# A hybrid decoder trunk on one Trainium2 core: rotary halves exchanged by GpSimd's DMAs, the decay from an exponential, the head norm from columns

## What is computed

```python
proj = rmsnorm(x, g) @ w_in       # rnn_gate, rnn_in, q, k, v, g_a, g_b: 7 x 1024 columns
u = causal_depthwise_conv(rnn_in)
r, i_gate = sigmoid(u @ w_a + b_a), sigmoid(u @ w_x + b_x)
a = exp(-8 * r * softplus(-lam))
h = scan(a, sqrt(1 - a * a) * i_gate * u)
y_a = h * gelu(rnn_gate)
# per head, q and k: t * cos + concat(-t[32:], t[:32]) * sin
w = softmax(q1 k1) - lam * softmax(q2 k2)      # 8 heads
y_b = rmsnorm(w @ v, g_sub) * (1 - lambda_init)   # norm over the head's 128
merged = sigmoid(g_a) * (y_a @ w_proj_a) + sigmoid(g_b) * (y_b @ w_proj_b)
x = x + rmsnorm(merged @ w_out, g1)
```

## Time and profile before

| | |
|---|---|
| median of 3 runs | 1862.76 us (1862.08 to 1863.0) |
| the profiled execution's own time | 1862.89 us |
| its span in the profile | 1861.2 us |
| PE busy | 1808.3 us, 97% of the span |
| DVE busy | 1541.8 us, 83% |
| ACT busy | 1307.3 us, 70% |
| POOL busy | 80.6 us, 4% |

### The profile page before, as it was taken

How to read it: one execution, slowest core, us unless ns; L and a number is a source line. 1 busy time by engine, 2 the same in 40 slices (tenths; PEclk the granted TensorE clock), 3 DMA queues, 4 the chain that set the end, 5 groups by cost and what they waited for, 6 DMA issues and landing times.

```text
span 1861.2 us, 29663 instructions
## 1 busy us (share of the span) xinstructions
PE 1808.3 (97%) x10489; PEld 1573.7 (85%) x10489; DVE 1541.8 (83%) x1973; ACT 1307.3 (70%) x1730; POOL 80.6 (4%) x73
## 2 busy tenths in 40 slices
PE   6999999999999999999999999999999999999997
PEld 6998999999879988987888888888888888888785
DVE  7898877666468898768998989989899888998996
ACT  6656646444467557547878888788888887888776
POOL 1000000000010000002001000010000000000300
PEclk9999999999999999999999999999999999999999
DMA  9543456555554443557999999999999999999991
GB/s 304 161 159 130 165 172 201 183 181 198 197 173 144 160 159 114 182 194 222 390 381 385 378 372 386 368 380 380 372 387 365 382 386 366 385 372 378 391 365 54
DMA packets 274002, 512.82 MB, mean 276 GB/s; under 512 B 9731, under 2 KB 113029, under 8 KB 273925
## 3 DMA queue, kind: packets, MB, share of 16 engines
q1 hardware_dynamic: 268400, 493.81, 74.6%
q0 software_dynamic: 5200, 17.86, 2.8%
q10 hardware_dynamic: 324, 0.12, 0.0%
HBM read 503.87 MB, written 7.88 MB: 275 GB/s over the span
## 4 chain that ended last, share of the span: by engine, by line
PE 82%; DVE 11%; ACT 6%; issue 2%; DMA 0%; SPq 0%; DVEq 0%; ACTq 0%
PE bank L1743 77%; DVE wlo L1093 4%; ACT whi L630 2%; PE bank L2198 1%; DVE T L1191 1%; PE bank L1898 1%; ACT SC L803 1%; ACT SQJ L641 1%; DVE SC L1227 1%; DVE RIN L1200 0%; ACT HH L688 0%; PE bank L2208 0%; ACT SC L798 0%; PE bank L1854 0%; ACT L731 0%
## 5 line engine op out<-in xcount | busy, mean ns | idle before, releaser
L630 ACT ACTIVATE whi<-raw 128x1024 fp32r<-128x1024 f32 x880 | 920.4, 1059 | 330.7 <-PE bank L1743 322.4
L1093 DVE TENSOR_TENSOR wlo<-raw,whi 128x1024 fp32r<-128x1024 f32 x880 | 1030.2, 1222 | 127.1 <-ACT whi L630 123.7
L1743 PE MATMUL bank<-HH,whi 128*128 128x256 f32 x1296 | 372.6, 287 | 3.0 <-DVE HL L1256 3.0
L1743 PE MATMUL bank<-HL,whi 128*128 128x256 f32 x1296 | 362.4, 280 | 0.0
L1743 PE MATMUL bank<-HH,wlo 128*128 128x256 f32 x1296 | 362.3, 280 | 0.0
L1743 PE MATMUL bank<-whi,XGH 128*128 128x512 f32 x896 | 358.4, 400 | 1.4 <-DVE wlo L1093 1.0
L1743 PE MATMUL bank<-whi,XGL 128*128 128x512 f32 x896 | 352.2, 393 | 0.0
L1743 PE MATMUL bank<-wlo,XGH 128*128 128x512 f32 x896 | 348.9, 389 | 0.0
L1743 PEld LDWEIGHTS bank<-HH,whi 128*128 128x128 f32 x1296 | 244.1, 188 | 7.5 <-issue 6.9
L1743 PEld LDWEIGHTS bank<-HL,whi 128*128 128x128 f32 x1296 | 244.4, 189 | 3.5 <-issue 2.9
L1743 PEld LDWEIGHTS bank<-HH,wlo 128*128 128x128 f32 x1296 | 246.3, 190 | 0.0
(11 more groups left out here) (348 smaller groups left out, 2123.4 us busy)
## 6 DMA issues: line engine op xcount, KB each, us to landing
raw<-in_moe_w_gate_dram SPq DMA_DIRECT2D x112, 1024.0 KB, 7.3
raw<-in_moe_w_up_dram SPq DMA_DIRECT2D x112, 1024.0 KB, 7.9
raw<-in_moe_w_down_dram SPq DMA_DIRECT2D x112, 1024.0 KB, 6.5
raw<-in_w_in_dram SPq DMA_DIRECT2D x56, 1024.0 KB, 5.1
raw<-in_ffn_w_gate_dram SPq DMA_DIRECT2D x14, 1024.0 KB, 5.0
raw<-in_ffn_w_up_dram SPq DMA_DIRECT2D x14, 1024.0 KB, 5.0
raw<-in_ffn_w_down_dram SPq DMA_DIRECT2D x14, 1024.0 KB, 4.9
raw<-in_w_proj_a_dram SPq DMA_DIRECT2D x8, 1024.0 KB, 5.2
```

The source lines that it names most:

```text
L630: nc.scalar.activation(whi[b % SPL][:, r], raw[b % RAW][:, r], ACT.Copy).then_inc(s_hi, 1)
L1093: v.tensor_tensor(wlo[b % SPL][:, r], raw[b % RAW][:, r], whi[b % SPL][:, r].bitcast(F32), ALU.subtract).then_inc(s_lo, 1)
L1743: ins = mm(dst, a, b, start=start and n == 0, stop=stop and n == 2, skip_group_check=True)
```

## The change

- `swap` goes. GpSimd waits until ACT has copied tile i of q or k into `QT` (now three buffers), and issues four transfers of 32 rows x 2 KB, each to the rows of the other half, into `QW` (four buffers in the space of `RIN`). The minus sign is in the sine table: `SIN` is taken with a scale `SGN` of +1 or -1 for each row, which GpSimd builds with three selects. `rotate` reads `QW` in place of PSUM and moves one block later, to blocks 6 to 13.
- The recurrence: tanh goes to a tile of its own (`TH`, in the space of `K`), the decay is an exponential of the gate (`decays`, ACT blocks 7 and 8), and the input factor is (1 + decay) times the root of the tanh. The tile-wise reciprocals (L1191) and ACT's two affine steps (L786, L791) go.
- The head norm: `head_square` becomes two products with the squared head output as weights and one column of `ONES` as data, so that the sums lie in 16 columns of one bank. One root of 128 x 16 (ACT block 25), one reciprocal (DVE block 25), and then `head_rows` on PE after chunk 26: 16 transposes of a column spread over 128, which gives the row form in banks 4 to 7. `normalise_heads` reads those, in blocks 26 and 27, and the splits follow in blocks 27 to 29. The copies into `MSALL`, the eight reciprocals (L1334) and the two roots of 128 x 1024 (L836) go.

The counters and waits of all this are changed to match, and `SPNEG` is one more small product in DVE's `constants`.

```diff
--- before.py
+++ after.py
@@ -139,13 +139,15 @@
         SGA = at("SGA", o_sga, [P, KT, SEQ])
-        QT = at("QT", o_sga, [P, 2, 2, SEQ])
-        QS = at("QS", o_sga + 4 * KB, [P, 2, SEQ])
+        QT = at("QT", o_sga, [P, 3, 2, SEQ])
+        QW = at("QW", o_rin, [P, 4, 2, SEQ])
...
         assert top <= end, (top, end)
-        OALL, MSALL = Q, K
+        OALL, TH = Q, K
+        SPNEG = SM[:, 72:88]
+        HSD, HRS = SM[:, 0:16], SM[:, 16:32]
@@ -498,15 +500,14 @@
                       allow_small_or_imprecise_dtypes=True).then_inc(s_pool, 1)
-            pool.wait_ge(s_pool, 10)
+            pool.wait_ge(s_pool, 9)
...
-            sw = SWAP[:, :].rearrange("p (g h j) -> p g h j", g=2, h=2)
-            pool.affine_select(out=sw[:, :, 0, :], in_=sw[:, :, 0, :], compare_op=ALU.not_equal, fill=-1.0, base=-32,
-                               pattern=[[-64, 2], [-1, 32]], channel_multiplier=1).then_inc(s_pool, 1)
-            pool.affine_select(out=sw[:, :, 1, :], in_=sw[:, :, 1, :], compare_op=ALU.not_equal, fill=1.0, base=0,
-                               pattern=[[-64, 2], [-1, 32]], channel_multiplier=1).then_inc(s_pool, 1)
+            for n, (row, fill) in enumerate(((96, -1.0), (64, 1.0), (32, -1.0))):
+                pool.wait_ge(s_sgn, n + 1)
+                pool.affine_select(out=SGN[:, :], in_=SGN[:, :], compare_op=ALU.is_ge, fill=fill, base=-row,
+                                   pattern=[[0, 1]], channel_multiplier=1).then_inc(s_sgn, 1)
@@ -520,6 +521,21 @@
             gates(0)
+
+            def exchange(layer):
+
+                for i in range(8):
+                    n = 8 * layer + i
+                    pool.wait_ge(s_eva, eva(layer, 4 + i))
+                    if i < 4:
+                        pool.wait_ge(s_u, 4 * layer + 4)
+                    else:
+                        pool.wait_ge(s_qr, n - 3)
+                    for q in range(4):
+                        r, other = 32 * q, 32 * (q ^ 1)
+                        pool.dma_start(QW[r:r + 32, i % 4, :, :], QT[other:other + 32, i % 3, :, :]).then_inc(s_qs[i % 4], 16)
+
+            exchange(0)
@@ -536,6 +552,7 @@
             gates(1)
+            exchange(1)
@@ -698,7 +715,8 @@
             act.wait_ge(s_r0, 1)
-            nc.scalar.activation(SIN[:, :], TT[:, 0, :], ACT.Sin).then_inc(s_r1, 1)
+            act.wait_ge(s_sgn, 4)
+            nc.scalar.activation(SIN[:, :], TT[:, 0, :], ACT.Sin, scale=SGN[:, 0:1]).then_inc(s_r1, 1)
@@ -746,8 +764,15 @@
                         act.wait_ge(s_c2, 1)
-                    ins = nc.scalar.activation(T2[:, t, :], T2[:, t, :], ACT.Tanh, scale=SPLAM[:, col:col + 1])
-                    ins.then_inc(s_ga, 1)
+                    nc.scalar.activation(TH[:, t, :], T2[:, t, :], ACT.Tanh,
+                                         scale=SPLAM[:, col:col + 1]).then_inc(s_ga, 1)
+
+            def decays(layer, g):
+
+                for t in range(4 * g, 4 * g + 4):
+                    col = layer * KT + t
+                    ins = nc.scalar.activation(T2[:, t, :], T2[:, t, :], ACT.Exp, scale=SPNEG[:, col:col + 1])
+                ins.then_inc(s_al, 1)
@@ -759,9 +784,9 @@
                         n = 8 * layer + i
-                        if i >= 2:
-                            act.wait_ge(s_qr, n - 1)
-                        nc.scalar.activation(QT[:, i % 2, :, :], bank2(c % 3), ACT.Copy).then_inc(s_eva, 1)
+                        if i >= 3:
+                            act.wait_ge(s_qr, n - 2)
+                        nc.scalar.activation(QT[:, i % 3, :, :], bank2(c % 3), ACT.Copy).then_inc(s_eva, 1)
@@ -781,14 +806,9 @@
                         act.wait_ge(s_iu, layer + 1)
-                        nc.scalar.activation(SQ[:, :, :], T2[:, :, :], ACT.Sqrt).then_inc(s_sq, 1)
-                    if c == 7:
-                        nc.scalar.activation(T2[:, :, :], T2[:, :, :], ACT.Copy, bias=1.0).then_inc(s_den, 1)
-                    if c in (12, 16):
-                        g = (c - 12) // 4
-                        act.wait_ge(s_bl, KT * layer + 4 * g + 4)
-                        r = T2[:, 4 * g:4 * g + 4, :]
-                        nc.scalar.activation(r, r, ACT.Copy, bias=-1.0, scale=2.0).then_inc(s_al, 1)
+                        nc.scalar.activation(SQ[:, :, :], TH[:, :, :], ACT.Sqrt).then_inc(s_sq, 1)
+                    if c in (7, 8):
+                        decays(layer, c - 7)
@@ -823,19 +843,12 @@
                         nc.scalar.activation(OSQ[:, h % 2, :], B[7][:, 0:SEQ], ACT.Square).then_inc(s_oc, 1)
-                    h = c - 18
-                    if 0 <= h < HEADS:
-                        n = HEADS * layer + h
-                        act.wait_ge(s_om, n + 1)
-                        nc.scalar.activation(MSALL[:, h, :], B[3][:, 0:SEQ], ACT.Copy, bias=EPS,
-                                             scale=1.0 / P).then_inc(s_oe, 1)
-                    if c == 28:
-                        act.wait_ge(s_or, HEADS * (layer + 1))
-                        for g in range(2):
-                            r = MSALL[:, 4 * g:4 * g + 4, :]
-                            nc.scalar.activation(r, r, ACT.Sqrt).then_inc(s_os, 1)
-                    if c in (29, 30):
-                        g = c - 29
+                    if c == 25:
+                        act.wait_ge(s_om, HEADS * (layer + 1))
+                        nc.scalar.activation(HSD[:, :], B[3][:, 0:2 * HEADS], ACT.Sqrt, bias=EPSC[:, 0:1],
+                                             scale=1.0 / P).then_inc(s_os, 1)
+                    if c in (27, 28):
+                        g = c - 27
@@ -1185,12 +1198,12 @@
                 if i == 0:
-                    dve.wait_ge(s_den, layer + 1)
...
                     dve.wait_ge(s_iu, layer + 1)
-                link(v.reciprocal(T2[:, i, :], T2[:, i, :]))
-                link(v.scalar_tensor_tensor(out=SQ[:, i, :], in0=SQ[:, i, :], scalar=2.0, in1=T2[:, i, :],
-                                            op0=ALU.mult, op1=ALU.mult))
+                if i % 4 == 0:
+                    dve.wait_ge(s_al, 2 * layer + i // 4 + 1)
+                link(v.scalar_tensor_tensor(out=SQ[:, i, :], in0=T2[:, i, :], scalar=1.0, in1=SQ[:, i, :],
+                                            op0=ALU.add, op1=ALU.mult))
@@ -1210,10 +1223,11 @@
                 cos, sin = (t[:, :].unsqueeze(1).to_broadcast([P, 2, SEQ]) for t in (COSR, SINR))
-                dve.wait_ge(s_qs, n + 1)
-                v.tensor_tensor(QS[:, :, :], bank2(6), sin, ALU.mult)
-                link(v.tensor_tensor(dst, QT[:, i % 2, :, :], cos, ALU.mult))
-                v.tensor_tensor(dst, dst, QS[:, :, :], ALU.add).then_inc(s_qr, 1)
+                turned = QW[:, i % 4, :, :]
+                dve.wait_ge(s_qs[i % 4], 64 * (2 * layer + i // 4 + 1))
+                v.tensor_tensor(turned, turned, sin, ALU.mult)
+                link(v.tensor_tensor(dst, QT[:, i % 3, :, :], cos, ALU.mult))
+                v.tensor_tensor(dst, dst, turned, ALU.add).then_inc(s_qr, 1)
@@ -1245,10 +1259,12 @@
             def normalise_heads(layer, g):
-                ms, o = (t[:, 4 * g:4 * g + 4, :] for t in (MSALL, OALL))
-                dve.wait_ge(s_os, 2 * layer + g + 1)
-                v.scalar_tensor_tensor(out=o, in0=o, scalar=GSUB[:, layer:layer + 1], in1=ms, op0=ALU.mult,
-                                       op1=ALU.mult).then_inc(s_yf, 1)
+                dve.wait_ge(s_hr, 2 * layer + g + 1)
+                for i in (4 * g, 4 * g + 2):
+                    o = OALL[:, i:i + 2, :]
+                    ins = v.scalar_tensor_tensor(out=o, in0=o, scalar=GSUB[:, layer:layer + 1], in1=bank2(4 + i // 2),
+                                                 op0=ALU.mult, op1=ALU.mult)
+                ins.then_inc(s_yf, 1)
@@ -1292,8 +1309,8 @@
                         tables_scaled(layer)
-                    if 5 <= c < 13:
-                        rotate(layer, c - 5)
+                    if 6 <= c < 14:
+                        rotate(layer, c - 6)
@@ -1328,14 +1345,13 @@
                                                op0=ALU.add, op1=ALU.mult).then_inc(s_evd, 1)
-                    if 19 <= c < 27:
-                        h = c - 19
-                        dve.wait_ge(s_oe, HEADS * layer + h + 1)
-                        v.reciprocal(MSALL[:, h, :], MSALL[:, h, :]).then_inc(s_or, 1)
+                    if c == 25:
+                        dve.wait_ge(s_os, layer + 1)
+                        v.reciprocal(HRS[:, :], HSD[:, :]).then_inc(s_or, 1)
+                    if c in (26, 27):
+                        normalise_heads(layer, c - 26)
                     if c in (28, 29):
-                        normalise_heads(layer, c - 28)
-                    if c in (30, 31):
-                        split_heads(layer, c - 30)
+                        split_heads(layer, c - 28)
@@ -1899,13 +1915,6 @@
-            def swap(layer, i):
-                n = 8 * layer + i
```

(39 more changed lines are left out.)

## The result

The changed kernel takes 1865.87 us (median of 19 runs, 1865.12 to 1868.38), the kernel before on the same chip 1863.14 (19 runs, 1861.59 to 1864.51). The ratio is 1.0016 with a 95% interval of 1.0009 to 1.0023: 3 us slower, where 15 us faster was forecast. The forecast's range ended at 1857.

A forecast was written before the change was run, and what follows sets the result against it. The prediction took PE to set the pace in the rotary stretch, with DVE close behind. Its terms, -13.6 + 2.4 + 3.5 + 0.3 - 6.4 - 3.0 + 1.8, sum to -15.0 us: 1847.8 us by the median, range 1839 to 1857.

The forecast's parts named there:

- The step that failed: Opening part: nothing outside the mixers is touched, so whatever PE saves in a mixer, the end comes earlier by.
- rival A: The forecast itself, the sum of all terms: 1847.8 us, own range 1842 to 1853, chance 0.64.
- The swap goes: Rotary stretch of the mixers: sixteen swaps leave PE, 0.85 us each, -13.6 us.
- slower chunks: Chunks behind a swap lose the quick step of 5.45 to 5.47 us: 14 at 0.17 us, +2.4 us.
- The waits: Attention chunks: PE's waits for AMX, SC and WT shrink to 2.1 us in each mixer, -6.4 us together.
- `HL`: Head split moves to blocks 27 to 29, so chunk 32 finds it done in both mixers: -3.0 us.
- `head_square`: Head norm on PE: four one-column passes, 0.47 us, replace two of 256 columns, 0.43; sixteen make +0.3 us.
- `head_rows`: After chunk 26 on PE: 32 transposes in all at 0.11 us, +3.5 us, with their input's preparation hidden.
- One table more: Residual norm's root must load its table, 1.28 us, 0.37 covered: 0.91 in each mixer, +1.8 us.
- The exchange is hidden: Rotary stretch: GpSimd's four transfers take 9.4 us a tile, under 11.9 us of cover; cost nothing.
- Rival B: GpSimd's issues, chunks 4 to 13, held back by DVE to 1.90 us each; exchange sets pace, 1872 us, chance 0.08.
- its account of DVE: Rotary stretch: without six reciprocals DVE needs 4.4 us a chunk against PE's 5.6, so it keeps pace without the swap.

The follow-up runs named there:

- the first run: The changed kernel with 480 bytes left free behind SGN, so every tile behind it keeps its address of before: 1843.47 us, ratio 0.9901 to the kernel before.

## Why the prediction was wrong

**The step that failed** is in its first part: "I carry the rest of the kernel over as it is: whatever PE saves in a mixer, the end comes earlier by." It rested on the code outside the mixers being untouched. But one edit, `SWAP` to `SGN`, moved every activation relative to the weights, and TensorE reads both in every matmul. Measured, the slower steps cost 0.0115 of the time, 21.4 us. By the two executions' chains (the changed kernel against the first run): experts 16.5 us (1012.8 against 996.3 from their start), dense layer 2.1, and the two mixers with their neighbourhood 2.1 and 3.5, which with 0.8 the other way between them is the 23.4 us between these two spans. That the unexplained two steps of 5.45 and 5.66 stood in the earlier trace rows should have warned me: I priced them at 2.4 us for 14 chunks, and not for the 5628 matmuls of the dense layer and the experts.

**The sum of the rest** was -15.0 and came out at -18.4 (ratio 0.9901) with the addresses restored, 1843.47 us, inside the own range of rival A. By parts:

- *The swap goes, -13.6, and slower chunks, +2.4*: -11.2 for the exchange. Measured 8.4 when it is added last, and 0 when added first. A swap cost 0.86, so -13.6 was right. The slower chunks reach further than the 14 priced: with the swap (all but the exchange) 40 of 51 unbroken runs of at least 20 matmuls ahead of the experts have the quick step, without it (the first run) 17 of 41. Outside the dense layer the mean step goes from 114.94 to 116.45 ns over some 3300 matmuls, 5.0 us, and 13.7 - 5.0 is 8.7. Against the kernel before (28 of 51, 116.01 ns) it is 1.5 us.
- *The waits, -6.4, `HL`, -3.0, `head_square`, +0.3*, with head rows and table together -3.8. Measured -10.1 without the exchange. The waits of the two mixers fell by more than forecast there, from 6.0 and 5.3 to 1.8 and 2.2 (5.3 with an `SC` of 0.7 in the second mixer that the earlier trace rows leave out), -7.3; `head_square` costs 0.34 in place of 0.43, -1.4 and not +0.3: four passes at 0.085 us, where the prediction held that one could hardly be under 0.118. With `HL` -3.0, `head_rows` +3.5 and 1.3 more for `X` this makes -6.9. The quicker steps, 116.01 to 114.94 ns over some 3250 matmuls, are 3.5 us more, and -10.4 is as near as one execution of each tells.
- *All together*, in the first run: swaps -13.7, steps +1.5, waits from 11.3 to 4.9 -6.4, `HL` -3.0, `head_rows` +3.5, `head_square` -1.4, `X` +0.9 make -18.6, against -18.4 measured. The 3.6 by which this beats the forecast are `head_square` (1.7), steps and table (0.9 each) and the swap's 0.1. That the waits come to the forecast's -6.4 is luck: an `SC` of 0.7 was left out, and 2.5 and 2.4 us stayed where 2.1 and 2.1 were forecast.
- *`head_rows`, 1.76 for 16*: 1.75, without a wait ahead of it.
- *One table more, 0.91 each*: the wait for `X` is 0.6 in the first mixer, and removing it gains nothing that can be measured.
- *The exchange is hidden*: yes, with smaller numbers than assumed, 0.49 us for each issue against 0.68 and a landing of 4.8 against 6.7. Rival B did not come: its 1.90 us for an issue stayed at 0.49, beside a DVE that was busy for 82% of 64 to 110 us. By *SBUF — State Buffer* of the Trainium skill, § Who interferes with whom, DVE's tensor_tensor leaves descriptor writing alone; the trace agrees. The landing of a 64 KB transfer is a median of 2.4 us in the kernel with the exchange alone and 4.8 in the changed one, with the 16 DMA engines busy for 0.75 and 0.79 of 64 to 110 us; why it doubles is not shown. By *DMA: Bandwidth & Descriptors* of the Trainium skill, § Anatomy of one DMA, it would be 2.2, an estimate from its figures: near the first and half of the second.

The two halves are worth 0 and 10.1 us apart and 18.4 together: without the swap DVE's reciprocals would have set the pace, and that they go is what lets the exchange pay. The forecast had this in its account of DVE (4.4 us for each chunk), but no price for either half alone.

## What to carry to other kernels

A buffer that is removed or shrunk moves everything laid out behind it: lay its bytes out as padding first and change one thing at a time, or the layout's effect is read as the change's. Where a profile shows a matmul of one form at two steps, time the layouts of that kernel (32 to 64 bytes are enough to turn it) before tuning anything that promises less than 1%. And where a change takes work from two engines that run close together, price the halves alone as well: the first one may be worth nothing.

## What the runs showed of the hardware

- TensorE's step depends on how the tiles in SBUF lie to one another, at the same granted clock: 10.91, 11.01 or 11.20 us for 48 matmuls of 512 columns, 218.36, 224.02 or 226.11 us for the dense layer's 1596. 32 unused bytes cost 21.4 us of 1863. That it is the distance between the two operands of a matmul is inferred. *SBUF — State Buffer* of the Trainium skill, § Who interferes with whom, gives TensorE two independent read ports and says that it never waits on anyone. For other engines the trace agrees (1228 of 1228 steps at 120 ns beside a DVE and an ACT that come and go); but the layout matters in spite of it, and there the measurement decides. Why was not found: nothing in the traces shows what a matmul does within its step.
- With the same addresses of activations and weights the dense layer took 218.36 us in two profiled kernels and 224.02 in others. Unbroken runs of 256-column matmuls keep one of two steps, 113.3 or 117.8 ns, from their first few matmuls to their end. What chooses is open.
- Within a wait of 4.3 us of TensorE the granted clock fell; it read 0.50 over 4.5 us behind the wait, which made the next chunk 1.6 us longer.
- GpSimd issued a 64 KB transfer within SBUF every 0.49 us beside a DVE that was busy for 82 to 87% of 64 to 110 us, with two-operand instructions for the most part.
